# An SSD mixer with its inner work and output projection one or two groups later in TensorE's program, and its time-step unit first

## What is computed

```python
def ssd_mixer(x, w_in, conv_w, conv_b, dt_bias, a_log, d_skip, norm_w, w_out):
    zxbcdt = x @ w_in                      # z 2048, xbc 4096, dt 64 columns
    xbc = silu(depthwise_conv(xbc, conv_w) + conv_b)     # 5 taps
    xs, bm, cm = split(xbc)                # 32 heads x 64; 8 groups x 128 twice
    dt = softplus(dt_raw + dt_bias); a_coef = -exp(a_log)
    y = run_ssd(forward) + run_ssd(backward) + d_skip * xs
    y = y * silu(z)
    return grouped_rmsnorm(y, norm_w) @ w_out            # 8 groups of 256
```

## Time and profile before

| | |
|---|---|
| median of 3 runs | 1638.13 us (1638.08 to 1642.66) |
| span of the profiled execution | 1636.2 us |
| PE, DVE, ACT, POOL busy | 93%, 62%, 47%, 19% of the span |
| first SSD mixer | from about 15 to 305 us |
| second SSD mixer | from about 1149 to 1442 us |
| granted TensorE clock, mean | 0.960 |

### The profile page before, as it was taken

How to read it: one execution, slowest core, us unless ns; L and a number is a source line. 1 busy time by engine, 2 the same in 40 slices (tenths; PEclk the granted TensorE clock), 3 DMA queues, 4 the chain that set the end, 5 groups by cost and what they waited for, 6 DMA issues and landing times.

```text
span 1636.2 us, 25496 instructions
## 1 busy us (share of the span) xinstructions
PE 1519.2 (93%) x10189; PEld 1404.6 (86%) x10189; DVE 1014.6 (62%) x1123; ACT 772.8 (47%) x1075; POOL 315.9 (19%) x386
## 2 busy tenths in 40 slices
PE   6999998999998989999689989999899999899998
PEld 5989897899988979998578779998888898789996
DVE  4778877645557475456434365546787878655545
ACT  3666675344434325443245434443475675525441
POOL 1434434000000000000456300000134433300000
PEclk9989998999999999999889989999989999799999
DMA  8637654355555455555799545555665655435552
GB/s 247 208 127 210 189 158 142 121 187 177 188 187 190 162 180 174 188 206 180 145 153 121 98 136 184 177 200 161 205 209 150 188 153 193 141 105 178 189 201 77
DMA packets 200757, 277.44 MB, mean 170 GB/s; under 512 B 12280, under 2 KB 168336, under 8 KB 200640
## 3 DMA queue, kind: packets, MB, share of 16 engines
q1 hardware_dynamic: 188032, 237.53, 43.9%
q0 software_dynamic: 11760, 37.96, 12.1%
q10 hardware_dynamic: 848, 0.32, 0.1%
HBM read 274.59 MB, written 1.18 MB: 169 GB/s over the span
## 4 chain that ended last, share of the span: by engine, by line
PE 46%; DVE 8%; ACT 5%; issue 2%; DMA 2%; POOL 1%; SPq 0%; DVEq 0%; ACTq 0%; POOLq 0%
PE y L647 19%; PE acc L526 16%; PE acc L539 5%; PE inner L783 2%; ACT w_high L953 2%; DVE conv L1391 2%; DVE w_low L1263 2%; DMA raw<-in_na_w_qkv 1%; PE inner L855 1%; DMA E<-cumsum_dram 1%; PE y L539 1%; ACT E L1047 1%; PE inner L875 1%; PE inner L616 0%; ACT E L1200 0%
## 5 line engine op out<-in xcount | busy, mean ns | idle before, releaser
L1263 DVE TENSOR_TENSOR w_low<-raw,w_high 128x2048 fp32r<-128x2048 f32 x226 | 517.6, 2300 | 173.3 <-ACT w_high L953 138.6
L526 PE MATMUL acc<-xT,w_high 128*128 128x256 f32 x3328 | 616.1, 287 | 3.4 <-DVE ring_c L1403 2.7
L526 PEld LDWEIGHTS acc<-xT,w_high 128*128 128x128 f32 x3328 | 530.5, 195 | 10.7 <-issue 3.0
L953 ACT ACTIVATE w_high<-raw 128x2048 fp32r<-128x2048 f32 x226 | 426.7, 1897 | 207.1 <-PE y L647 75.4
L526 PE MATMUL acc<-xT,w_low 128*128 128x256 f32 x1664 | 474.6, 285 | 0.0
L647 PE MATMUL y<-w_high,opT 128*128 128x512 f32 x1408 | 403.7, 396 | 18.4 <-DVE opT L1411 13.6
L647 PEld LDWEIGHTS y<-w_high,opT 128*128 128x128 f32 x1408 | 262.9, 191 | 74.8 <-issue 23.5
L526 PEld LDWEIGHTS acc<-xT,w_low 128*128 128x128 f32 x1664 | 323.2, 194 | 0.0
L647 PE MATMUL y<-w_low,opT 128*128 128x512 f32 x704 | 225.0, 393 | 0.0
L1279 DVE TENSOR_TENSOR opT<-conv,opT 128x512 fp32r<-128x512 f32 x56 | 38.8, 693 | 270.5 <-issue 245.1
L539 PE MATMUL acc<-w_high,xT 128*128 128x256 f32 (+1 forms) x960 | 184.3, 294 | 9.1 <-DVE xT L1324 9.1
(11 more groups left out here) (137 smaller groups left out, 1264.4 us busy)
## 6 DMA issues: line engine op xcount, KB each, us to landing
raw<-in_ffn_w_in SPq DMA_DIRECT2D x128, 512.0 KB, 4.7
raw<-in_ffn_w_out SPq DMA_DIRECT2D x128, 512.0 KB, 4.4
raw<-in_ssd_w_in SPq DMA_DIRECT2D x96, 512.0 KB, 5.2
E<-cumsum_dram POOLq DMA_DIRECT2D x32, 512.0 KB, 5.8
raw<-in_ssd_w_out SPq DMA_DIRECT2D x32, 512.0 KB, 5.5
raw<-in_sc_w_in SPq DMA_DIRECT2D x24, 512.0 KB, 4.7
raw<-in_na_w_qkv SPq DMA_DIRECT2D x24, 512.0 KB, 6.5
E<-cumsum_dram POOLq DMA_DIRECT2D x32, 256.0 KB, 6.3
```

The costliest lines, as they stand in the source:

```text
L526: mm = nc.tensor.matmul(bank[:, c * SEQ:(c + 1) * SEQ][:, span], w[:, col:col + P], xT[:, k, low, span], start=(k == 0 and part == 0), sto ...
L953: nc.scalar.activation(w_high[:, u % SPLIT, 0:k * c], raw[:, u % RAW, 0:k * c], ACT.Copy).then_inc(w_high_done, 1)
L1263: V.tensor_tensor(w_low[:, u % SPLIT, 0:k * c], raw[:, u % RAW, 0:k * c], f(w_high[:, u % SPLIT, 0:k * c]), ALU.subtract).then_inc(w_low_d ...
```

## The change

No arithmetic changes. Four programs are reordered: `dt` becomes the first unit of the mixer; on PE `cumsum_rows` goes behind the first x unit, `turn_xs` behind bc, `turn_gated` behind x, and the output units come four groups behind the projections instead of two, so that so(i-4) stands in group i. The last four output units stand after the last projections. On ACT the decays of group i-1 are now done in group i, on both sides of `squares(i-2)`; `copy_xs` goes behind the tanh of bc and `gated_high` behind that of x. On DVE `gated_low` goes behind `silu_x`. On POOL the load of the next E goes ahead of `rms_power`. SP's queue of weights follows `plan_units`. The diff, with ACT and DVE cut to the middle groups:

```diff
@@ plan_units
+SO_LAG = 4
...
-            for g in range(G + 2):
+            add(names, "dt", j, 0)
+            for g in range(G):
                 if g < G - 1:
                     add(names, "z", j, g)
-                if g == 0:
-                    add(names, "dt", j, 0)
-                if g < G:
-                    add(names, "bc", j, g)
-                    add(names, "x", j, g)
-                if g == G - 1:
-
-                    add(names, "z", j, g)
-                if g >= 2:
-                    add(names, "so", j, g - 2)
+                add(names, "bc", j, g)
+                add(names, "x", j, g)
+                if g >= SO_LAG:
+                    add(names, "so", j, g - SO_LAG)
+            add(names, "z", j, G - 1)
+            for g in range(G - SO_LAG, G):
+                add(names, "so", j, g)
@@ POOL
-                    for g in range(G - 1):
+                    scale_xs(0)
+                    skip_xs(0)
+                    for g in range(1, G - 1):
+                        load_decays(g + 1)
+                        rms_power(g - 1)
                         scale_xs(g)
-                        if g >= 1:
-                            rms_power(g - 1)
-                            load_decays(g + 1)
                         skip_xs(g)
-                        if g >= 1:
-                            mask_decays(g + 1)
+                        mask_decays(g + 1)
@@ TensorE
-                    head_units(s, [names[("z", 0)], names[("dt", 0)]])
+                    head_units(s, [names[("dt", 0)], names[("z", 0)]])
...
                     project(names[("bc", 0)], range(NT))
                     cumsum()
+                    project(names[("x", 0)], range(NT))
                     cumsum_rows()
-                    project(names[("x", 0)], range(NT))
                     for i in range(1, G - 1):
                         project(names[("z", i)], range(NT))
-                        if i <= 2:
-
-                            project(names[("bc", i)], range(NT))
-                        turn_xs(i - 1)
                         if i >= 2:
                             scan(i - 2)
                         state_products(i - 1)
-                        if i > 2:
-                            project(names[("bc", i)], range(NT))
-                        if i > 2:
+                        project(names[("bc", i)], range(NT))
+                        turn_xs(i - 1)
+                        project(names[("x", i)], range(NT))
+                        if i >= 2:
                             turn_gated(i - 2)
-                        project(names[("x", i)], range(NT))
-                        if i == 2:
-                            turn_gated(i - 2)
-                        if i >= 2:
-                            out_unit(s, names[("so", i - 2)], first=(i == 2))
+                        if i >= SO_LAG:
+                            out_unit(s, names[("so", i - SO_LAG)], first=(i == SO_LAG))
 
                     project(names[("bc", G - 1)], range(NT))
-                    turn_xs(G - 2)
                     scan(G - 3)
                     state_products(G - 2)
                     project(names[("x", G - 1)], range(NT))
+                    turn_xs(G - 2)
+                    out_unit(s, names[("so", G - 5)])
                     turn_gated(G - 3)
                     project(names[("z", G - 1)], range(NT))
                     scan(G - 2)
+                    state_products(G - 1)
                     turn_xs(G - 1)
-                    out_unit(s, names[("so", G - 3)], between=lambda: state_products(G - 1))
+                    out_unit(s, names[("so", G - 4)])
                     turn_gated(G - 2)
                     scan(G - 1)
+                    out_unit(s, names[("so", G - 3)])
                     out_unit(s, names[("so", G - 2)], between=lambda: turn_gated(G - 1))
@@ ScalarE, the middle groups as they are now
                     for i in range(1, G - 1):
                         z_tanh(i)
+                        if i >= 2:
+                            decays(i - 1, early)
                             squares(i - 2)
+                            decays(i - 1, late)
                             normalise(i - 2)
                         start_conv("bc", i)
                         conv_tanh()
+                        copy_xs(i - 1)
                         start_conv("x", i)
...
                         conv_tanh()
                         if i == 1:
                             decays(0, late)
+                        else:
+                            gated_high(i - 2)
@@ VectorE, the middle groups as they are now
                     for i in range(1, G - 1):
                         silu_z(i)
+                        if i >= 2:
                             gate_scan(i - 2)
                             decayed_products(i - 1)
+                        silu_bc(i, taps("bc", i))
                         silu_x(i, taps("x", i))
                         if i == 1:
                             decayed_products(0)
+                        else:
+                            gated_low(i - 2)
```

More of the change, by code:

```diff
@@ L1114, in _ @@
                                          scale=-1.0).then_inc(ncs_done, 1)
+                    conv_tanh()
+                    start_conv("x", 0)
                     act.wait_ge(cs_rows, mixer + 1)
@@ L1127, in _ @@
                             normalise(i - 2)
                         start_conv("bc", i)
-                        if i > 2:
-                            gated_high(i - 2)
-                        else:
-                            copy_xs(i - 1)
-                        if i <= 2:
-                            decays(i - 1, early)
-                        if i == 2:
-                            decays(1, late)
                         conv_tanh()
-                        if i == 2:
-                            squares(0)
-                            normalise(0)
-                            gated_high(0)
+                        copy_xs(i - 1)
@@ L1142, in _ @@
                         start_conv("x", i)
                         if i == 1:
+                            decays(0, early)
+                        conv_tanh()
+                        if i == 1:
                             decays(0, late)
-                        if i > 1:
-                            decays(i, early)
-                        conv_tanh()
-                        if i > 1:
-                            decays(i, late)
-                    start_conv("bc", G - 1)
+                        else:
+                            gated_high(i - 2)
@@ L1151, in _ @@
+                    decays(G - 2, early)
+                    start_conv("bc", G - 1)
+                    conv_tanh()
+                    decays(G - 2, late)
+                    squares(G - 3)
+                    start_conv("x", G - 1)
+                    normalise(G - 3)
                     copy_xs(G - 2)
                     conv_tanh()
-                    squares(G - 3)
-                    normalise(G - 3)
-                    start_conv("x", G - 1)
                     gated_high(G - 3)
-                    conv_tanh()
+                    z_tanh(G - 1)
```

42 lines of the change are left out of this document (15 added, 27 removed).

## The result

The changed kernel takes 1683.4 us in the median (1678.35 to 1687.88 in 4 runs) against 1639.2 (1638.08 to 1642.66) for the kernel before in the same session: ratio 1.0264, interval 1.0240 to 1.0289. It is **44 us slower**. The forecast was 1668, slower by 30; direction and range held, the size was too small by 14.

The account below looks back on a forecast made before the run. The prediction took a closed chain over DVE and ACT as the bound, not PE. Start, middle groups and end (8.9 + 4.3 + 5 first mixer, 2.6 + 4.3 + 5 second) added 30.1 to 1638.1: 1668 us, range 1643 to 1688.

Parts of the forecast that it names:

- What bounds the kernel: In the mixer's groups, a closed chain over DVE and ACT sets 31.4 us; PE follows with about 1 us slack.
- The middle groups: Groups with four splits cost 33.6 us instead of 31.4, groups 3 and 4 have one split less: +4.3 us per mixer.
- The hole: In each middle group DVE stands idle 3.9 us before its products, waiting for the late decays on ACT.
- The start: Up to the x taps of group 2: 8.9 us later in the first mixer, 2.6 in the second.
- 6 us later: At the mixer's start, the DMA storing the cumsum rows begins at 50.6, moving E's loads, masks and `scale_xs(0)` on POOL.
- The end: From a middle group's last x taps to the last output unit: 66.3 us instead of 61.7, +4.6, taken as 5.
- The walk: Step-by-step timing of the end from the last middle group's x taps at 0 to the last output unit at 66.3.
- scan 7 (53.9): Step near the mixer's end: the last scan, after products 7, low half and split at 51.6, done at 53.9.
- A: Rival: PE is the bound and its waits of 13.6 and 16.2 us go: 1608, or 1623 for half; chance 0.12.
- B: Rival: POOL's work falls elsewhere and 28 DVE taps save 0.75 each, 21 us back: 1645 or 1636; chance 0.08.
- C: Rival: PE's longer waits keep its clock low, up to 24 us over six groups in two mixers: 1685 to 1692; chance 0.12.
- `turn_gated` of group 5: Sign expected in the changed profile: on PE this step comes after a wait over 5 us.

Follow-up runs that it names:

- Experiment 3: Kernel before, with ACT making the high halves of the next weights ahead of the late decays: 1626.12 us, ratio 0.9919.
- experiment 6: Changed kernel with the cumsum rows turned, copied and stored as early as before: 1688.19 us, ratio 1.0285 to the kernel before.
- experiment 5: Changed kernel with group 2 alone in the order of before (bc 2 projected ahead of scan 0): 1661.67 us, ratio 1.0128 to the kernel before.
- Experiments 8 and 9: Both in the changed kernel. 8: output unit of group 5 ahead of turn_gated(6) and scan 7, 1670.93 us. 9: output units three groups behind, not four, 1671.73 us.
- experiment 4: Kernel before with only the output units moved, four groups behind instead of two: 1664.52 us, ratio 1.0156.

## Why the prediction was right in direction and too small

**What bounds the kernel: right.** Experiment 3 moved nothing on PE or DVE, and the kernel fell by 0.8% with PE's waits. The Trainium skill, Perfetto Trace Analysis, section Identifying the Most-Contended Engine, sends one first to the engine of the highest share, and judges TensorE by its rate of arithmetic and the busy share of its weight loads rather than by that of its matmuls. Both shares are highest on PE in the kernel before (weight loads 86%, matmuls 93%). The trace disagrees there: an edit on ACT, at 47%, gave 11 to 13 us. In experiment 3's middle groups PE is busy 30.0 of 30.0 us; that PE is the engine to work on next is argued, no run takes work off it.

**The middle groups: right in mechanism, a little too dear.** The hole was 3.82 us for 3.9, the group of four splits 33.4 for 33.6. Forecast +4.3 a mixer, measured +2.7 and +1.1, because the groups of before were not all 31.4: those of its second mixer took 31.5 to 32.1, by the spacing of the x silus.

**The start: the place right, one step wrong.** The step that the rows' DMA comes "**6 us later**, and both loads of E, both masks and `scale_xs(0)` behind them on POOL move with it" failed. The DMA did come 7.7 us later (52.24 for 44.54), but the delay ran out on POOL. POOL's mask of group 0 began 4.2 us later (64.50 for 60.31) but took 3.10 us for 6.50, and `scale_xs(0)` hadn't moved; experiment 6 moves the rows forward and gains nothing. What releases the first scan is DVE's products at 83.01 for 80.18, late, by ACT's rows, because the late decays of group 0 now stand behind the tanh of x 1. That delay was +2.8, not +4.3. No run moves these decays alone, so their part is read from the trace. The rest of the term, nothing to cover the wait and bc 2's taps behind the gate, held: group 2 took 42.3 us for 33.2, and experiment 5 gave 11 and 10 back. That the sum came near is partly luck. In the first mixer the scan began 1.5 us sooner than forecast, took 10.6 for 8.4, and what stands behind it took 25.1 for 23.4: +11.3 for +8.9. In the second mixer the same walk was out by the same amounts, 1.1 sooner, then 2.2 and 1.7 too short: +5.4 for +2.6. The 8.4 was the first mixer's scan of the kernel before, at a mean clock of 0.62; its second mixer's, which took 10.6 us, I had not looked at.

**The end: mis-sized, +5 for +13.1 and +11.1.** It makes 14.2 of the 14.6 us by which the mixers were missed. It is nearly all of the miss only because two others cancel, which is luck: the start was 5.2 us dearer than forecast in the two mixers together, the middle groups 4.8 cheaper. The walk held to 1 us up to the last products (they end 49.3 us behind the x taps of group 6, forecast 48.4), with the x taps of group 7 at 7.11 for 4.0 and other steps a little shorter. Then "scan 7 (53.9)" counted 5.5 us for the scan. It took 10.4 at the 1.2 GHz level (+4.9), behind `turn_gated(6)`, 0.9 us that the walk left out. The trace before had warned of it: there, behind a wait of 2.08 us, scan 7 took 8.7 us at a mean of 0.59. The last gate was due at 53.9 and came at 60.9, and what follows took 13.9 for 12.4, its output unit beginning at the slow clock. I had charged PE's clock with 0.4 us in all. Experiments 8 and 9 put scan 7 at full clock and make the end 8.7 and 6.1, and 10.2 and 8.8 us shorter; in both that is the clock together with an output unit less behind the scan, and no run parts the two.

**The rivals.** A (PE bound, waits go) fell: the waits went and the time rose. B (ports relieve DVE) came true in part: bc taps took 3.25 for 4.0, but x taps, beside POOL's skip product (2.97) and mask (3.13), took 5.53, so the sum of all taps in the run rose from 129.4 to 139.1 us. C (the slow clock joins the chain) did not act in the middle groups, as said, but at the end it did, which my 0.12 on "six groups" had not looked at; experiment 4 shows it in middle groups once the output unit is gone. `turn_gated` of group 5 did not wait over 5 us: `turn_xs(6)` ahead of it took the wait, 6.62, for the `inner` bank that gate 5 still held.

## What to carry to other kernels

When two engines pass work to each other in a closed loop, look on their own timelines for idle time before each hand-over, and move what nobody waits for behind what somebody does: one line on ACT gave 0.8%, while putting PE's output units later, in experiment 4, lost 1.6%. Before moving a piece on the busiest engine, ask what it covered, since a long independent piece between a producer and its consumer is worth its cover (experiments 4, 5, 8). Cost the work behind a new wait of several microseconds at the slow clock, above all a long chain of small matmuls that somebody waits for.

## What the hardware showed that I had not expected

- The scan of 64-column matmuls takes 5.4 to 5.6 us at granted clock 1.00 and 10.3 to 10.7 at 0.50. Behind waits of PE of 4.27, 5.38, 6.41 and 10.99 us it ran at 0.50, and so it did behind 2.89 in the second mixer of the kernel before; behind 0.96 it ran at 1.00. Behind 3.32 and 2.50 with 2.05 us of matmuls between, 0.50 too; in the first mixer of the kernel before, behind 1.57 and 2.08, 0.62 and 0.59 in the mean of the scan. What decides between the two levels these runs don't settle.
- Eight taps on DVE take 3.25 us alone, 5.53 where the end of POOL's skip product and its mask run, and 7.11 where two scalings, the product and the mask stand beside them. POOL can lose too: its skip product took 2.97 us, most of it beside the split that DVE does ahead of the taps, for 1.04 elsewhere. Beside the taps of 7.11 its three products took 1.18, 1.22 and 1.10. The Trainium skill, SBUF — State Buffer, section Who interferes with whom, says that a DVE instruction with two SBUF inputs contends with a GpSimd one that reads SBUF; the trace agrees, by 2.3 us for eight taps.
